# Keys of the latent attention projected feature-major, and the shared rotary key turned once for all heads

## The reference

```python
def _mla_group(cq, ckv, kr, q_norm, kv_norm, w_uq, w_uk, w_uv, cos, sin):
    q = (_rmsnorm_2(cq, q_norm) @ w_uq).reshape(B, S, MLA_HEADS, MLA_NOPE + MLA_ROPE)
    q_nope = q[..., :MLA_NOPE]
    q_rope = _rope(q[..., MLA_NOPE:], cos[:, :, None, :], sin[:, :, None, :])
    c = _rmsnorm_2(ckv, kv_norm)
    k_nope = (c @ w_uk).reshape(B, S, MLA_HEADS, MLA_NOPE)
    v = (c @ w_uv).reshape(B, S, MLA_HEADS, MLA_VDIM)
    k_rope = _rope(kr, cos, sin)
    ...
        s = (jnp.einsum('bqhd,bkhd->bhqk', qn, k_nope)
             + jnp.einsum('bqhr,bkr->bhqk', qr, k_rope)).astype(jnp.float32) * scale
```

## Time and profile before

| | us |
|---|---|
| Time of the kernel, median of 3 runs | 995.21 (995.01 to 996.04) |
| Time of the profiled execution | 997.04 |
| Its span, first to last instruction | 995.2 |
| TensorE busy | 983.3 |
| VectorE busy | 672.6 |
| ScalarE busy | 593.6 |

### The profile page before, as it was taken

The page is one execution under the profiler, slowest core; times in us unless marked ns, Lnnn a source line. Parts: engine busy times, 40 slices in busy tenths (PEclk is TensorE's granted clock), DMA queues, the critical chain, the costliest instruction groups (busy, mean ns, idle before and its releaser), DMA issues.

```text
span 995.2 us, 18822 instructions
## 1 busy us (share of the span) xinstructions
PE 983.3 (99%) x8050; PEld 890.0 (89%) x8050; DVE 672.6 (68%) x896; ACT 593.6 (60%) x829; POOL 25.4 (3%) x26
## 2 busy tenths in 40 slices
PE   8999999999999999999999999999999999999996
PEld 7899987888989999998899999889899999987985
DVE  5675688867755788875556565785695556588565
ACT  7677576574537656654446676537754765654581
POOL 0000000000000000000000003000000000130000
PEclk9999999999999999999999999999999999999999
DMA  8762434656565665557654553553556446534331
GB/s 297 270 200 92 150 115 161 210 170 205 176 193 191 187 192 171 170 169 253 190 156 148 147 173 115 163 158 129 172 168 193 151 118 190 170 129 142 137 128 42
DMA packets 97283, 166.45 MB, mean 167 GB/s; under 512 B 6896, under 2 KB 32240, under 8 KB 96816
## 3 DMA queue, kind: packets, MB, share of 16 engines
q1 hardware_dynamic: 95792, 159.18, 50.7%
q0 software_dynamic: 976, 4.46, 1.3%
q10 hardware_dynamic: 432, 1.62, 0.4%
HBM read 164.19 MB, written 1.05 MB: 166 GB/s over the span
## 4 chain that ended last, share of the span: by engine, by line
PE 94%; DVE 2%; ACT 2%; issue 1%; DMA 1%; SPq 0%; DVEq 0%; ACTq 0%
PE proj L623 14%; PE proj L624 14%; PE proj L625 14%; PE proj L632 13%; PE proj L634 13%; PE proj L633 13%; PE mix L668 1%; PE mix L944 1%; PE mix L693 1%; PE mix L676 1%; PE mix L905 1%; PE mix L893 1%; DMA raw<-in_w_mem_kv 1%; ACT arena L1372 1%; PE mix L701 1%
## 5 line engine op out<-in xcount | busy, mean ns | idle before, releaser
L1532 DVE TENSOR_TENSOR wlo<-raw,whi 128x1024 fp32r<-128x1024 f32 (+2 forms) x304 | 356.6, 1202 | 177.3 <-ACT whi L1067 176.0
L1067 ACT ACTIVATE whi<-raw 128x1024 fp32r<-128x1024 f32 (+2 forms) x304 | 307.3, 1040 | 185.4 <-PE proj L634 81.3
L623 PE MATMUL proj<-act_hi,whi 128*128 128x256 f32 x1064 | 304.0, 286 | 0.5 <-ACT arena L1345 0.5
L624 PE MATMUL proj<-act_lo,whi 128*128 128x256 f32 x1064 | 301.0, 283 | 0.0
L625 PE MATMUL proj<-act_hi,wlo 128*128 128x256 f32 x1064 | 301.0, 283 | 0.0
L623 PEld LDWEIGHTS proj<-act_hi,whi 128*128 128x128 f32 x1064 | 203.2, 191 | 3.0 <-ACT arena L1345 1.4
L624 PEld LDWEIGHTS proj<-act_lo,whi 128*128 128x128 f32 x1064 | 203.3, 191 | 0.5
L625 PEld LDWEIGHTS proj<-act_hi,wlo 128*128 128x128 f32 x1064 | 203.2, 191 | 0.2
L632 PE MATMUL proj<-whi,y_hi 128*128 128x512 f32 (+1 forms) x340 | 133.3, 392 | 1.3 <-DVE wlo L1532 1.3
L634 PE MATMUL proj<-whi,y_lo 128*128 128x512 f32 (+1 forms) x340 | 132.3, 389 | 0.0
L633 PE MATMUL proj<-wlo,y_hi 128*128 128x512 f32 (+1 forms) x340 | 132.3, 389 | 0.0
(11 more groups left out here) (335 smaller groups left out, 1027.4 us busy)
## 6 DMA issues: line engine op xcount, KB each, us to landing
raw<-in_w_in SPq DMA_DIRECT2D x144, 512.0 KB, 4.4
raw<-in_w_up SPq DMA_DIRECT2D x88, 256.0 KB, 4.4
raw<-in_w_out SPq DMA_DIRECT2D x32, 512.0 KB, 3.5
raw<-in_w_down SPq DMA_DIRECT2D x22, 512.0 KB, 5.7
raw<-in_w_mem_k SPq DMA_DIRECT2D x8, 512.0 KB, 4.0
raw<-in_w_o SPq DMA_DIRECT2D x8, 512.0 KB, 3.9
raw<-in_w_mem_v SPq DMA_DIRECT2D x8, 512.0 KB, 4.1
raw<-in_w_mem_kv SPq DMA_DIRECT2D x7, 512.0 KB, 6.7
```

Source lines behind the costliest of these rows:

```text
L623: mm(o, wh[:, i, wc], hi[:, k0 + i, :], start=begin and j % 2 == 0, stop=False, skip_group_check=True)
L624: mm(o, wh[:, i, wc], lo[:, k0 + i, :], start=False, stop=False, skip_group_check=True)
L1067: fn(whi[c % SPLIT][:, 0:w], raw[c % SLOTS][:, 0:w], ACT.Copy).then_inc(s.w_hi, 1)
L1532: tt(wlo[c % SPLIT][:, 0:w], raw[c % SLOTS][:, 0:w], f32(whi[c % SPLIT][:, 0:w]), ALU.subtract).then_inc(s.w_lo, 1)
```

## The change

uk becomes a feature-major projection. Its result has two heads on each tile of 128 partitions, features 0 to 63 of the even head on partitions 0 to 63 and those of the odd head on 64 to 127. ScalarE copies it straight into `LKT`, in two copies of 64 partitions and 1024 elements, one for the even and one for the odd heads. `LK` is gone, and the rotation on VectorE no longer waits for uk nor copies the key into the heads. The shared key is transposed once for each block, out of a 96-column slice of `CK` that ends with its 32 rotated features, so that they land on partitions 64 to 95 of bank 3 of `mix`. ScalarE copies these 32 partitions into all 8 heads of `LKT`, in two copies that read the 256 elements four times over. The queries' transposes of heads 6 and 7 go to the same bank and wait for those two copies.

```diff
-FEATURE_MAJOR = ("if", "sbq", "sbk", "mlq", "mlk", "up", "memk", "memq", "memg", "mlag", "hgf", "hgq", "hgg")
+FEATURE_MAJOR = ("if", "sbq", "sbk", "mlq", "mlk", "up", "memk", "memq", "memg", "mlag", "uk", "hgf", "hgq", "hgg")
...
-                pool.wait_ge(s.mla_t, 8 * L + 8)
+                pool.wait_ge(s.mla_t, 5 * L + 5)
...
                 pe.wait_ge(s.mla_r, L + 1)
-                for n, src in enumerate((LQ, LK)):
-                    for h in range(MLA_H):
-                        if n and h % 2 == 0:
-                            pe.wait_ge(s.mla_tk, 8 * L + h // 2 + 1)
-                        for b in range(NB):
-                            last = nc.tensor.transpose(mix[0:QK_D, h // 2, (h % 2) * SEQ + b * P:(h % 2) * SEQ + (b + 1) * P], src[:, b, h, :], ident)
-                        if h % 2:
-                            last.then_inc(s.mla_t, 1)
+                for b in range(NB):
+                    last = nc.tensor.transpose(mix[0:QK_D, 3, b * P:(b + 1) * P], CK[:, b, Q_RANK + KV_RANK - NOPE:], ident)
+                last.then_inc(s.mla_t, 1)
+                for h in range(MLA_H):
+                    if h == 6:
+                        pe.wait_ge(s.mla_tk, 6 * L + 2)
+                    for b in range(NB):
+                        last = nc.tensor.transpose(mix[0:QK_D, h // 2, (h % 2) * SEQ + b * P:(h % 2) * SEQ + (b + 1) * P], LQ[:, b, h, :], ident)
+                    if h % 2:
+                        last.then_inc(s.mla_t, 1)
                 project("hgf1", L, act_hi, act_lo)
...
-                pe.wait_ge(s.mla_tk, 8 * L + 8)
+                pe.wait_ge(s.mla_tk, 6 * L + 6)
+                pe.wait_ge(*out_of("uk", L))
                 scores(0)
...
                 act.wait_ge(*done("uk", L))
-                for b in range(NB):
-                    last = fn(LK[:, b, :, 0:NOPE], bank("uk", L)[:, b, :].rearrange("p (h d) -> p h d", h=MLA_H), ACT.Copy)
+                for n in range(2):
+                    last = fn(LKT[0:NOPE, :, :].rearrange("p (j n) t -> p j n t", n=2)[:, :, n, :], tiles("uk", L)[n * NOPE:(n + 1) * NOPE, :, :], ACT.Copy)
...
-                for n, dst in enumerate((LQT, LKT)):
-                    for pr in range(4):
-                        act.wait_ge(s.mla_t, 8 * L + 4 * n + pr + 1)
-                        fn(dst[0:QK_D, 2 * pr:2 * pr + 2, :], mix[0:QK_D, pr, :].rearrange("p (h t) -> p h t", h=2), ACT.Copy).then_inc(s.mla_tk, 1)
+                act.wait_ge(s.mla_t, 5 * L + 1)
+                for four in range(2):
+                    fn(LKT[NOPE:QK_D, 4 * four:4 * four + 4, :], over(mix[NOPE:QK_D, 3, 0:SEQ], 4), ACT.Copy).then_inc(s.mla_tk, 1)
+                for pr in range(4):
+                    act.wait_ge(s.mla_t, 5 * L + pr + 2)
+                    fn(LQT[0:QK_D, 2 * pr:2 * pr + 2, :], mix[0:QK_D, pr, :].rearrange("p (h t) -> p h t", h=2), ACT.Copy).then_inc(s.mla_tk, 1)
...
-                for name in ("uqa", "uqb", "uk"):
+                for name in ("uqa", "uqb"):
                     dve.wait_ge(*out_of(name, L))
...
-                    link(tt(k2, v[2], v[3], ALU.add))
-                    last = copy(LK[:, b, :, NOPE:QK_D], over(t, MLA_H))
+                    last = tt(k2, v[2], v[3], ALU.add)
+                    if b == 0:
+                        link(last)
                 last.then_inc(s.mla_r, 1)
```

More of the change, by code:

```diff
@@ L489, in stack_kernel @@
         MP, MPT = ar(6144, 8, SEQ), ar(8192, 8, SEQ)
-        LQ, LK = ar(1024, NB, MLA_H, QK_D), ar(2560, NB, MLA_H, QK_D)
+        LQ = ar(1024, NB, MLA_H, QK_D)
         LV, LGT = ar(4096, NB, 512), ar(5120, 4, SEQ)
```

## The result

| | before | after |
|---|---|---|
| Time, median of 6 runs each (us) | 995.00 (994.36 to 996.04) | 998.22 (997.21 to 1000.92) |
| Ratio | | 1.0037, interval 1.0023 to 1.0052 |
| Profiled execution: time, span | 997.04, 995.2 | 998.07, 996.3 |
| TensorE busy | 983.3 | 979.4 |

The changed kernel is 0.37% slower, 3.2 us between the medians, where 0.09% was forecast. It lies above the range, and above the 997.2 us from which the forecast counts a result as slower.

What follows compares the result with a forecast made beforehand. TensorE, busy 983.3 of 995.2 us, was taken to bound the kernel. +0.90 and -0.43 us per layer gave +0.94 for two layers, added to the median 995.21: forecast 996.15 us, range 994.4 to 997.5.

Steps and rivals of the forecast that it cites:

- Part 1: Projection uk on TensorE: 6 matmuls of 512 columns become 12 of 256, costing 0.04 us, which vanish in a longer hold.
- Part 2: ScalarE's two copies emptying uk's bank grow from 1.08 to 1.98 us and delay hgf0: +0.90 us per layer.
- Part 3: Rotation on VectorE gets about 0.5 us shorter; worth zero, with 4.6 us of cover before the first transpose.
- Part 4: 14 fewer transposes, but the last 4 wait for two ScalarE copies of the turned key: -0.43 us per layer.
- B: Rival: only the broadcast copies are cheap, at 256 elements' price; -0.59 us per layer, 994.0 us; chance 0.04.
- C: Rival: broadcast-source or upper-to-lower-partition copies cost more than their elements; a doubled key pair gives 1000.1 us; chance 0.07.
- A: Rival: the holds cost nothing, only instruction counts matter; -1.45 us per layer, 992.3 us in all; chance 0.03.
- D: Rival: transposes cost 0.275 us each, with no hold among them; -2.95 us per layer, 989.3 us; chance 0.01.
- The sum: Both edited places together: +0.47 us per layer, +0.94 for two layers, added to the median 995.21 us.
- a displaced wait elsewhere: Case within the chance of a slower result: a wait displaced outside the edited places; chance 0.02.
- nothing else moved: Sign expected in the changed kernel's profile: apart from the listed changes at uk, hgf0 and the transposes, no movement.
- The warning on the clock: If the clock fell to 1.2 GHz behind hgf0's longer wait, later matmuls would take twice their spacing, the forecast far too low.

Runs made afterwards that it cites:

- after_again: The changed kernel repeated without any edit; 998.10 us, 1.0027 of the kernel before.
- before_pad64: The kernel before with 64 tiny matmuls (256 TensorE instructions, one whole block) added to the warm-up; 998.07 us, 1.0025 of the kernel before.
- before_pad56: The kernel before with 56 tiny matmuls (224 TensorE instructions, 32 short of a block) added to the warm-up; 998.64 us, 1.0034 of the kernel before.
- early_shared_warm5: early_shared with 5 instead of 10 of the larger warm-up matmuls (20 TensorE instructions fewer); 993.06 us, 0.9967 of the kernel before.
- the kernels with 8 pads: The changed kernel, alone or with further edits, with 8 tiny matmuls (32 TensorE instructions) added to the warm-up; 992.16 to 997.25 us.
- early_shared: early, with VectorE besides copying uk's even heads out of its bank while ScalarE copies the odd ones; 995.09 us, 0.9992 of the kernel before.
- early: The changed kernel with the last quarter of hgf0 moved behind the turned key's two transposes; 997.17 us, 1.0008 of the kernel before.

## Why the prediction was right and wrong

The step that failed is the claim that nothing moves but the two edited places, a term put at nothing without a reason. In its place the runs show a hold of TensorE of 1.9 us behind layer 1's first burst (1.8 to 2.6 us in the five profiles whose burst begins at record 186 or 188), which the changed length of TensorE's instruction stream brings about.

**What bounds the kernel: right.** Of the edits, those that added or took away a wait of TensorE showed in the time.

**Part 1, uk on TensorE: right.** 0.05 us for 0.04.

**Part 2, emptying uk's bank: right.** +0.96 us for +0.90, since the pair took 2.04 us for 1.98; part 1's 0.05 vanished in the hold, as told. Half the partitions made no copy shorter.

**Part 3, the rotation: right.** VectorE's next instruction behind it, a product of line 1907, begins at 586.99, 5.2 us ahead of the first transpose at 592.22.

**Part 4, the transposes: right in its mechanism, 0.19 us too careful.** The pair of broadcast copies started 0.42 after the first transpose as told, took 1.92 for 1.98, and the restart cost nothing. -0.62 for -0.43. The broadcast source and the shift from upper to lower partitions cost nothing that can be seen; rivals B and C fall by this row, and A with the hold of 0.70 itself. D falls too: sixteen transposes in 1.66 us are 0.104 each.

**The sum, first failure: the baseline.** "The median of the three runs shown is 995.21, 1.83 below the profiled one; the change adds the same to it." The edited code did add what was summed, 0.7 for 0.94. But the profiled execution stood above the median for a reason that I never looked for: its 1.6 us at half the clock. I treated two different distances as one kind. Time less span is 1.8 us in every execution (997.04 - 995.2, 998.07 - 996.3), and the difference of the profiled time from the median happened to be 1.83 as well. For the edit's own price this does no harm. It did hide the second failure in the profile: without the stretch the changed kernel's span should have come out 1.6 us lower, and it didn't.

**The sum, second failure: a term that isn't there.** The prediction counted what the edit does where it stands. The 16 instructions a layer that it takes from TensorE's stream were priced at their own duration; that they move every later burst against the blocks of 256 was not. The ledger gives +0.5, +2.1 and -0.8 us at the bursts, in sum **+1.8 us**. With it the account closes: 0.7 + 1.8 = 2.5 against a difference of 2.7 between the spans at full clock (995.8 and 993.1). Of the three only the +2.1 is shown to be the change's: the +0.5 is missing in after_again, and the hold of before that makes the -0.8 is missing in before_pad64, whose bursts lie at the same records. The difference of the medians, 3.2, holds 0.5 more. Half of the changed kernel's executions had a mean clock of 0.996 or less, so half-clock stretches are the likely source; for before, whose clocks are not on record here, it isn't shown. The 0.02 given to "a displaced wait elsewhere" was the right case with far too small a chance; "nothing else moved" was the claim that failed, and the list of waits of before has a last line marked issue (line 944, 0.4 us) that I passed over.

**The range.** "Runs of one kernel spread over 1.0 us" came from three runs. In the three sets the runs of before lie between 994.2 and 998.3. A range from the spread of three could not hold what belongs to the clock.

**The warning on the clock** came true at another hold. Behind hgf0's wait of 1.17 us the matmuls start 0.12 apart and the granted clock stays at 1.00. Behind the fetch hold it fell in two of five profiles.

## What to carry to other kernels

An edit that changes the number of instructions on TensorE moves the rest of its stream against the 16 KB blocks in which it is fetched; where the kernel has bursts of some hundred short instructions, look for waits marked issue right behind them, see in the DMA view whether they end just after a packet of the instruction queue has landed (here 1.2 to 1.5 us), and try a few tiny matmuls at the start before a verdict on an edit worth less than 2 us. Look at the granted clock of the profiled execution, stretch by stretch, before its span is set against a median. A count of operations removed is worth what the last wait behind them leaves: here 14 transposes of 0.107 us brought 0.62, and moving two of them ahead of independent matmuls brought the rest.

## What the runs showed of the hardware

**Instruction blocks of TensorE.** They come as 16 KB packets that mostly take 0.9 to 1.4 us, and no instruction of a block ran sooner than 1.21 us after it landed, in 870 cases. When a packet starts isn't fixed to the crossing into the block ahead of it: over the 14 profiles it starts between 4.8 us before that crossing and 3.8 us after it. That start decides about the hold more than the burst's place does. Bursts that begin at records 181 to 188, grouped by it:

| Bursts | packet starts, from the crossing | hold behind the burst, us |
|---|---|---|
| layer 0 of before_pad56 and early_shared_warm5, four | 1.2 to 0.5 before | none |
| layer 0's second of the kernels with 8 pads, four of six profiles | 0.6 to 0.5 before | none |
| the same burst in the other two of the six | 0.4 and 0.6 after | 0.7 |
| layer 1's first, five profiles | 1.6 to 2.4 after | 1.8 to 2.6 |

So the same place in a block is free in one row and costs 2 us in another, and the 8 pads bring layer 0's second burst to record 186, where it held in two of six profiles. In the after and before_pad56 traces the burst of layer 1 follows 33 records that start within 1.3 us, while the four bursts of the first row follow matmuls 0.12 or 0.23 us apart; that this makes the packet late is a guess. No run varies it, and the request for a packet is in no trace.

**The clock behind a hold.** Stretches of early_shared, behind its hold of 1.77 us that ended at 882.87:

```profile
880.00:883.00 3.00, 1.23 (x52) 0.93 (x39) 2.53 (x3) 2.23 (x3) 0.00 (x0) 1.00 0.25 93
883.00:886.00 3.00, 3.00 (x9) 2.33 (x9) 2.19 (x3) 0.00 (x0) 0.00 (x0) 0.61 0.79 235
886.00:889.00 3.00, 3.00 (x19) 2.75 (x18) 0.00 (x0) 1.06 (x1) 0.00 (x0) 0.83 0.80 292
```

TensorE stood, went on at 2.4 GHz for three matmuls, and then worked at 1.2 GHz for some seven. The same in before_pad56, where the starts go from 0.23 to 0.43 us apart (rows above). In after, after_again and early the same hold had no such sequel. So the stall at times costs more than its own length: in before_pad56 the eight slow starts add 1.6 us.

**A stretch at half the clock without any stall** at about 179 us, in 5 of the 14 profiles, with TensorE busy before and through it. What sets it off, no run here shows.

**Tiny matmuls at the start aren't free.** 56 and 64 of 32 columns cost 1.9 and 3.0 us by the starts named above.
